# A two-block transformer on one core: sixteen experts at fixed places, three-product weights of 1 MB, and a loop for what overflows

## What is computed

```python
g_logits = (t @ w_group) + b_group                       # 4 groups, the best one is taken
e_logits = ((t @ w_router) + b_router).reshape(-1, 4, 4)
top_p, top_i = lax.top_k(softmax(e_in), 2)               # 2 of the group's 4 experts
w = top_p / sum(top_p) * p_g
hid = silu(einsum('td,edf->etf', t, w_gate)) * einsum('td,edf->etf', t, w_up)
hid = hid * combine.T[:, :, None]
y = einsum('etf,efd->td', hid, w_down)                   # 16 experts: 1024 -> 512 -> 1024
```

## Time and profile before

| what | us |
|---|---|
| median of three executions (range) | 2140.98 (2139.52 to 2141.97) |
| the profiled execution | 2142.71 |
| its span, first to last instruction | 2141.1 |
| PE busy | 1881.8 (88%) |
| DVE busy | 687.8 (32%) |
| ACT busy | 646.3 (30%) |
| first expert product to last (604.5 to 960.5 in the chain) | 356 |

### The profile page before, as it was taken

One profiled execution on the slowest core, in us unless ns is written; L12 is line 12 of the kernel. 1 busy time (PEld: TensorE's weight loads), 2 busy tenths in 40 slices (PEclk: granted clock), 3 DMA queues, 4 the chain that ended last, 5 costly groups with the idle time before them and its releaser, 6 DMA issues.

```text
span 2141.1 us, 21791 instructions
## 1 busy us (share of the span) xinstructions
PE 1881.8 (88%) x8127; PEld 1362.9 (64%) x8127; DVE 687.8 (32%) x1233; ACT 646.3 (30%) x1140; POOL 279.3 (13%) x380
## 2 busy tenths in 40 slices
PE   5996999999479999994999999697777859999996
PEld 4883666667434444443888888585463648888885
DVE  3545334333200000104332332614443262322324
ACT  3224555642110100103221322422546232223222
POOL 2100532310100000001000000423506200000000
PEclk9997999999579999996999999898779879999998
DMA  5226532121279999965332332333000022323321
GB/s 181 83 82 221 189 110 81 60 79 50 93 274 325 344 328 343 325 243 196 99 98 89 99 98 88 97 93 104 1 29 11 30 69 79 98 89 99 99 98 50
DMA packets 210788, 279.53 MB, mean 131 GB/s; under 512 B 9554, under 2 KB 135073, under 8 KB 210576
## 3 DMA queue, kind: packets, MB, share of 16 engines
q1 hardware_dynamic: 198672, 244.35, 34.8%
q0 software_dynamic: 12032, 34.06, 4.4%
HBM read 241.12 MB, written 35.16 MB: 129 GB/s over the span
## 4 chain that ended last, share of the span: by engine, by line
PE 83%; DVE 7%; DMA 3%; issue 2%; POOL 2%; ACT 2%; SPq 0%; DVEq 0%; ACTq 0%; POOLq 0%
PE psum L366 19%; PE psum L367 18%; PE psum L368 18%; PE psum L1059 10%; PE psum L1073 5%; PE psum L505 3%; PE psum L523 3%; PE psum L494 2%; POOL arena L612 2%; DMA warea<-in_w_in 1%; DVE tarea_r L1575 1%; ACT warea_r L351 1%; DVE harea L1547 1%; PE psum L1051 1%; DVE harea L1562 1%
## 5 line engine op out<-in xcount | busy, mean ns | idle before, releaser
L357 DVE TENSOR_TENSOR warea_r<-warea,warea_r 128x2048 fp32r<-128x2048 f32 x114 | 266.5, 2339 | 410.4 <-ACT warea_r L351 410.3
L366 PE MATMUL psum<-tarea_r,warea_r 128*128 128x512 f32 x896 | 356.9, 398 | 12.6 <-DVE tarea_r L1575 12.6
L367 PE MATMUL psum<-tarea_r,warea_r 128*128 128x512 f32 x896 | 351.4, 392 | 0.0
L368 PE MATMUL psum<-tarea_r,warea_r 128*128 128x512 f32 x896 | 351.4, 392 | 0.0
L351 ACT ACTIVATE warea_r<-warea 128x2048 fp32r<-128x2048 f32 x114 | 217.6, 1910 | 308.9 <-PE psum L368 282.4
L1059 PE MATMUL psum<-warea,arena 128*128 128x512 f32 x512 | 225.6, 599 | 0.8 <-ACT arena L1404 0.7
L366 PEld LDWEIGHTS psum<-tarea_r,warea_r 128*128 128x128 f32 x896 | 169.7, 189 | 53.4 <-DVE tarea_r L1575 13.3
L368 PEld LDWEIGHTS psum<-tarea_r,warea_r 128*128 128x128 f32 x896 | 169.7, 189 | 36.4
L367 PEld LDWEIGHTS psum<-tarea_r,warea_r 128*128 128x128 f32 x896 | 169.9, 190 | 33.6
L1059 PEld LDWEIGHTS psum<-warea,arena 128*128 128x128 f32 x512 | 97.1, 192 | 118.2 <-issue 116.7
L366 PE MATMUL psum<-warea_r,tarea_r 128*128 128x512 f32 (+3 forms) x408 | 157.1, 385 | 1.4 <-DVE tarea_r L1953 1.4
(11 more groups left out here) (272 smaller groups left out, 2207.6 us busy)
## 6 DMA issues: line engine op xcount, KB each, us to landing
warea<-in_ffn_w_gu SPq DMA_DIRECT2D x88, 512.0 KB, 5.0
warea<-in_w_gate SPq DMA_DIRECT2D x32, 1024.0 KB, 7.9
warea<-in_w_up SPq DMA_DIRECT2D x32, 1024.0 KB, 7.8
warea<-in_w_down SPq DMA_DIRECT2D x32, 1024.0 KB, 7.1
warea<-in_w_in SPq DMA_DIRECT2D x48, 512.0 KB, 4.7
warea<-in_ffn_w_down SPq DMA_DIRECT2D x40, 512.0 KB, 4.2
x_slots<-arena SPq DMA_DIRECT2D x4, 3072.0 KB, 14.9
arena<-x_slots POOLq DMA_DIRECT2D x17, 512.0 KB, 7.7
```

Source lines behind the costliest of these rows:

```text
L357: dve.tensor_tensor(w_lo[:, u % 2, :], raw[:, u % RAW, :], w_hi[:, u % 2, :].bitcast(f32), ALU.subtract)\
L366: nc.tensor.matmul(out, high, by_high, start=first, stop=False)
L367: nc.tensor.matmul(out, high, by_low, start=False, stop=False)
L368: return nc.tensor.matmul(out, low, by_high, start=False, stop=last)
```

## The change

**Places.** Expert e has block e, whatever its count: slots 128e to 128e + 127. A token whose rank is beyond 128 goes to an overflow block behind the sixteen. `slot_of` and `over_of` are constants for that. Blocks 0 to 14 are written out in every engine's program (`STATIC` = 15) and need nothing from `isml`; block 15 and the overflow blocks are a loop from `STATIC` to `last`. With these inputs the loop runs once, so sixteen blocks are computed, as before.

**Weights.** Each expert is six units of 1 MB: two for gate, two for up, two for down. One DMA loads one unit, and a partition reads one piece of 8 KB (rows p*8 to p*8+3 of the matrix) in place of four of 2 KB. To match it the transposes read `Xb` and `hb` with a step of 8 and 4 elements. There are twelve raw places (`moe_raw`): four in the arena, the two `raw` buffers, four over `hT` and two over `hn`. SP issues units 0 to 3 when the first attention's last product is done, 4 and 5 behind the last units of `w_out`, 6 to 9 when the router's logits are done, 10 and 11 when the scatter is done, and every later one when the unit 12 before it is split. At the end SP waits for the split of unit 77 (`moe_lo` 78) and not for `y_stored` before it feeds the FFN.

**Products.** Every unit is split like the other weights, by ACT and DVE, into the same two buffers `w_hi` and `w_lo`; `XT` and the hidden block are split too. Each fp32 product becomes three of fp32r: a unit is 4 products, 12 matmuls, and a block 72. ACT's `moe_high` for unit n waits for the end of unit n - 2 on PE (`moe_done` n - 1). The copy of the result is shared: ACT the first half, DVE the second.

**Routing.** The counts come before the ranks on PE, the ranks take 4 products and not 10, the slots are signalled (`slots_ready`) before the experts of the overflow blocks, and DVE splits units 0 and 1 before it reads the counts.

The core of the diff:

```diff
-    moe_loaded = [s[f"moe_load{i}"] for i in range(RING)]
+    moe_in = [s[f"moe{i}"] for i in range(12)]
+    moe_raw = ([carve(7168 + 2048 * k, 2048) for k in range(4)] + [raw[:, k, :] for k in range(2)]
+               + [whole(HT_AT + 2048 * k, 2048) for k in range(4)] + [whole(H_AT + 2048 * k, 2048) for k in range(2)])
+    def moe_high(b, i):
+        act, parity = nc.scalar, i % 2
+        n, slot, fills = moe_unit(b, i)
+        act.wait_ge(moe_in[slot], 16 * fills)
+        if not (isinstance(n, int) and n < 2):
+            act.wait_ge(s["moe_done"], n - 1)
+        act.activation(w_hi[:, parity, :], moe_raw[slot], ACT.Copy).then_inc(s["moe_hi"], 1)
+
+    def moe_low(b, i):
+        dve.wait_ge(s["moe_hi"], n + 1)
+        dve.tensor_tensor(w_lo[:, parity, :], moe_raw[slot], w_hi[:, parity, :].bitcast(f32), ALU.subtract)\
+            .then_inc(s["moe_lo"], 1)
...
-            sp.wait_ge(s["y_stored"], 1)
+            sp.wait_ge(s["moe_lo"], 78)
             ffn_half(0, "ffn1", AT_FFN1)
...
-            pool.wait_ge(s["routed"], 1)
+            pool.wait_ge(s["slots_ready"], 1)
...
-            def gate_up(k, i=0):
-                for g in range(2):
-                    moe_arrived(pe, k + g, i)
-                    for c in range(KD):
-                        mm = nc.tensor.matmul(ps[g], XT[:, c, :], wv[:, c, :], start=c == 0, stop=c == KD - 1)
-                    mm.then_inc(s["gu_psum"], 1)
+            def gate_up(b):
+                pe.wait_ge(s["xt_low"], 2 * b + 2)
+                for i in range(4):
+                    n = moe_unit(b, i)[0]
+                    pe.wait_ge(s["moe_lo"], n + 1)
+                    for k in range(4):
+                        c = 4 * (i % 2) + k
+                        mm = products(ps[i // 2], XT_hi[:, c, :], XT_lo[:, c, :], w_hi[:, i % 2, 512 * k:512 * k + 512],
+                                      w_lo[:, i % 2, 512 * k:512 * k + 512], c == 0, c == KD - 1)
+                    mm.then_inc(s["moe_done"], 1)
...
+            def expert_round(b):
+                gate_up(b)
+                slot_features(b + 1)
+                if not (isinstance(b, int) and b == 0):
+                    down(b - 1, 4)
+                hidden_features(b)
```

More of the change, by code:

```diff
@@ L199, in build_blocks @@
     rstd = sb("rstd", [P, 32])
-    small = sb("small", [P, 1000])
+    small = sb("small", [P, 992])
     isml = sb("isml", [P, 64], i32)
@@ L701, in _, with expert @@
             sp.wait_ge(s["routed"], 1)
             last = last_block(sp)
[L703 to L710, removed]
+            def expert(b):
+                return sp.value_load(isml[0:1, ds(b - STATIC + 9, 1)], min_val=0, max_val=NE - 1)
@@ L711, in _ @@
+            with sp.Fori(STATIC, last + 1) as b:
                 e = expert(b)
-                expert_weights(5, "w_gate", e, (s["gu_psum"], 2 * b - 1))
-                expert_weights(6, "w_up", e, (s["gu_psum"], 2 * b))
+                for i in range(4):
+                    expert_unit(b, i, e)
                 before = expert(b - 1)
-                expert_weights(7, "w_down", before, (s["y_psum"], 2 * b - 2))
-            expert_weights(5, "w_down", expert(last), (s["gu_psum"], 2 * last + 1))
+                for i in range(4, 6):
+                    expert_unit(b, i, before)
@@ L718, in ffn_half @@
+            final = expert(last)
+            for i in range(2):
+                n, slot, _ = moe_unit(last + 1, i)
+                sp.wait_ge(s["moe_lo"], 6 * last + i)
+                src = w["w_down"][0][ds(final, 1), :, :].rearrange("o (p c) f -> p (o c) f", p=P)
+                sp.dma_start(moe_raw[slot].rearrange("p (c f) -> p c f", c=2), src[:, 2 * i:2 * i + 2, :])\
+                    .then_inc(moe_in[slot], 16)
             def ffn_half(g, name, at):
@@ new lines, in expert_round @@
+            def expert_round(b):
+                gate_up(b)
+                slot_features(b + 1)
+                if not (isinstance(b, int) and b == 0):
+                    down(b - 1, 4)
+                hidden_features(b)
+            slot_features(0)
+            for b in range(STATIC):
+                expert_round(b)
+            pe.wait_ge(s["routed"], 1)
+            last = last_block(pe)
+            with pe.Fori(STATIC, last + 1) as b:
+                expert_round(b)
+            down(last, 0)
@@ L1416, in _ @@
+                moe_high(b, 5 if zero else 7)
+                act.wait_ge(s["htr_psum"], b + 1)
+                nc.scalar.activation(HT_hi, ps[6].rearrange("p (c q) -> p c q", c=4), ACT.Copy).then_inc(s["hts_ready"], 1)
+                if not zero:
+                    y_high(b - 1, n0 + 6)
+            act.wait_ge(s["mix_psum"], 8)
+            for i in range(2):
+                moe_high(0, i)
+            slot_high(0)
+            for b in range(STATIC):
+                expert_round(b)
             act.wait_ge(s["routed"], 1)
-            slot_copy(0)
```

276 lines of the change are left out of this document (166 added, 110 removed).

## The result

| | before | after |
|---|---|---|
| median of the executions, us (range) | 2141.97 (2139.52 to 2144.29) | 2154.30 (2150.51 to 2155.5) |
| profiled execution, us | 2142.71 | 2150.51 |
| its span, us | 2141.1 | 2148.9 |
| granted clock | 0.931 | 0.931 |

Of five executions of after, one took 3158.22 us at a granted clock of 0.552 and is left out of its median, its range and the ratio. The ratio of after to before is 1.0056, 95% interval 1.0041 to 1.0071: slower by little, but clear of the noise. The forecast was 2134 us; the measured median is 20 us above it, inside the range of 2117 to 2163 and near the price of rival 1, 2157.

What follows compares the result with a forecast made beforehand. Plain fp32 products on PE were taken to bound the expert stage. Terms of -8, +7 and -6.6 us summed to -7.6, so a median of 2134 us, with an 8-in-10 range of 2117 to 2163.

Steps and rivals of the forecast that it cites:

- rival 1: Expert stage: the turn is longer than its links; at 7.8 us the kernel takes 2157 us; chance 0.26.
- What bounds the kernel now: Expert stage before the change: bound by plain fp32 products on PE, 21.91 us a block.
- term 2: Expert stage: the turn through two split buffers sets the pace, 363 us against 355.9, so +7 us.
- term 3: Way from the stage to the first FFN product: halved result copy and less traffic beside the gather, -6.6 us.
- term 1: Way to the first expert product: earlier routing, scatter running alone and landing at 586.5, block load 6 us; -8 us.
- the turn: Expert stage: loop of waits PE, ACT, DVE, PE through one split buffer, 7.31 us per two units, three a block.
- the ends: Ways into and out of the expert stage: -8 us to the first expert product, -6.6 us to the first FFN product.
- The transposes: Expert blocks on PE: reading columns 32 bytes apart costs nothing up to twice 1.3 us; at four times, +27 us.
- The fit: Gather before the FFN: the skill's 2.0 us + bytes / 436 GB/s gives 3.2 us for 512 KB.
- Rival 2: Expert stage: PE's clock falls in the gaps; a third of the stage at 1.2 GHz gives 2190 us; chance 0.08.
- Rivals 4 and 5: Ends of the stage: 4, they give more, turn 7.15, about 2119 us, chance 0.14; 5, nothing, about 2144, 0.10.
- Rival 3: Expert stage: PE sets the pace after all, 17.6 us a block, 2065 us; chance 0.04.

Runs made afterwards that it cites:

- e6: Changed kernel with sixteen blocks written out, no overflow loop, and one plain fp32 matmul per expert product, nothing split; 2129.4 us, ratio to before 0.9934.
- e14: e13 with its third pair of split buffers taken away and nothing else; 2145.1 us, ratio to before 1.0042.
- e7: Changed kernel with SP's first expert unit issued only when slots are known, and DVE's first two splits behind the routing; 2171.9 us, ratio to before 1.0129.
- e9: Changed kernel with DVE's first two splits of expert weights moved from ahead of the routing's arithmetic to behind it; 2151.6 us, ratio to before 1.0049.
- e2: Changed kernel with blocks written out, no overflow loop, and ten raw places in place of twelve; 2150.6 us, ratio to before 1.0064.
- e3: e2 with a third pair of split buffers; 2133.7 us, ratio to before 0.9981.
- e4: e3 with a second buffer for token blocks; 2128.5 us, ratio to before 0.9951.
- e12: e4 with eight gather buffers and DVE's first two splits moved behind the routing; 2125.1 us, ratio to before 0.9934.
- e13: e12 with GpSimd issuing each token block's load a block earlier, ahead of its wait for a result; 2075.4 us, ratio to before 0.9694.
- e10: Changed kernel with eight gather buffers in place of four, so no gather waits for an addition; 2149.3 us, ratio to before 1.0043.

## Why the prediction was wrong

**What bounds the kernel now** was right: plain products at 21.9 us a block in before, and e6, which keeps them, has a stage of 355.8 us.

**The steps that failed.** The forecast sum was -7.6 us and the traces gave +11.0. Of these 18.6 us, 11.2 lie in term 2, 4.3 in term 3 and 3.1 in term 1. With the turn well sized the sum would have been near nothing, -7.6 + 7.2 = -0.4; it takes the token block and the ends as well to come to the measured loss.

**Term 2, the turn mis-sized.** The mechanism was the right one, and so were three of the five links: 1.94, 2.29 and 2.51 us. The two handoffs at the ends of the ring were mis-sized: PE to ACT 732.34 - 731.85 = 0.49 us for 0.42, and DVE to PE's flowing matmuls 0.23 for 0.16: DVE ends at 736.57, PE starts at 736.72, and its second matmul comes at 737.03, 0.08 later than the pace of 0.23. The turn is 7.46 us for 7.31. The 0.42 had been read where ACT starts another instruction, one that reads PSUM, and the 0.05 in the 0.16 behind another of DVE's. The trace of before has the ring's own pairs, with the ring's own sizes: ACT's copy of a unit behind PE (1325.86 - 1325.37 = 0.49), and PE behind DVE's large subtraction, which ends at 183.25 + 2.29 = 185.54, 0.15 before PE starts.

```profile
1325.37 0.39 PE L368 MATMUL psum<-warea_r,arena_r 128*128 128x512 f32 x1
...
1325.86 1.92 ACT L351 ACTIVATE warea_r<-warea 128x2048 fp32r<-128x2048 f32 x1 [8.96 <-PE psum L368]
```

```profile
183.25 2.29 DVE L357 TENSOR_TENSOR warea_r<-warea,warea_r 128x2048 fp32r<-128x2048 f32 x1 [4.16 <-ACT warea_r L351]
...
185.69 0.30 PE L366 MATMUL psum<-warea_r,arena_r 128*62 128x256 f32 x1 [1.65 <-DVE warea_r L357]
```

So nothing in the changed kernel made the handoffs longer; they were read between the wrong pairs. 48 turns of 0.15 us are 7.2 us of the missing 11. About 3 us more are the token block, which the forecast had at no cost because DMA had "no more than now" to move: 374.3 us in after against 371.2 in e14. The remaining 1 us lies in the allowances for the ends. The stage, +18.2, is within the prediction's bounds, which were 8 below and 18 above its +7.

**Rival 1** came out near its price, and in part by luck. It named the deciding turn, 7.47 us, and the changed kernel's block of 22.58 is a turn of 7.53. But its 2157 us was a turn of 7.8 with the full gain at the ends; measured were a shorter turn and half that gain. Of its causes, small work in front of a copy and the strided transposes, e14 shows neither: with both in place its blocks are three turns of 7.46 us and nothing more. I gave it 0.26 because each engine had a third of its time free; but in a ring of waits spare time does not shorten the links.

**Term 1, right but for the load.** The scatter landed at 587.13, 586.5 was forecast, and e7 shows what the early fetch does for it. Counted from the router's first product, at 543.99 us before and 544.96 after, GpSimd starts 29.2 us behind it before and 28.5 after: 0.7 less, as forecast. What the prediction did not see is the room there: DVE's first two splits stand on the routing's path, and e9 and e6 put the worth of taking them away at 5 us of GpSimd's start. One size was off: the load of block 0 took 8.75 us, not 6. In e2, e3, e4, e12, e13 and e14, whose scatters landed 2 to 4 us later, it took 3.5 to 3.7. These have ten raw places, none of them over `hn`, so no unit is issued beside that load, and more units are issued ahead of it. The two exchange with each other, so neither alone says what the crowd costs.

**Term 3, wrong in its bound.** I took the gather as bound by bytes (5.7 us for 2.1 MB less). With the bytes gone, at 256 GB/s and a DMA share of 0.78, the time from the first gather's issue to the last sum's end fell from 20.8 us to 19.1 only. e10 takes the handshake away (eight pieces, four buffers, each reuse waiting for an addition) and has 17.5: eight issues one behind the other take 10.1 us up to the last, whose landing and sum add 7.4. So the issues, the last landing and the handshake were left as the bound. The halved copy gave 0.5 us of the 0.6 forecast.

**The transposes** were costed at nothing, and the Trainium skill's page "SBUF — State Buffer", Door 1, spoke of a penalty for each access that leaves a 16-byte line. In this trace there is hardly one. Eight transposes of after, columns 32 bytes apart, took 1.98 us at half clock (above); at full clock they start 0.111 us apart in after and 0.109 in before. Eight of before at half clock, columns side by side, from its chain of waits at the same place:

```profile
601.91 1.96 PE psum L1051 x8
```

**The fit** of "DMA: Bandwidth & Descriptors" (the Trainium skill, anatomy of a DMA), 3.2 us for 512 KB, was not reached by the gathers, 5.69 and 5.74 us. The store of the last result, alone, took less, 2.92 us. The nearest load is that of block 0 in e13, which took

```profile
591.31 3.47 DMA arena<-x_slots
```

**Rival 2** (the clock falls in the gaps) did not happen: gaps, mostly of 0.8 to 1.7 us, in nearly every turn, and a clock of 1.00. Rivals 4 and 5 are out: the ends gave 7.2 us, between the 20.6 and the 3 that they had, and the stage was not theirs. Rival 3 was true of a kernel a third pair of buffers, a second token block and one earlier issue away (e13, which has eight gather buffers as well).

**Slips in the sums** that changed nothing: two subtractions of DVE are 4.6 us in a turn and not 4.4, and two copies of ACT 3.8 and not 3.6.

## What to carry to other kernels

Where work goes round through several engines and a few buffers, add the links up, and read each handoff between the same pair of instructions that will pass work on in the new kernel: 0.07 us in two of them made 7 of the 18.6 us by which this forecast missed, and the right values stood in the trace of before. A third buffer cut this ring, and only then did the next limit show, a load that one queue issued behind a store; so after each limit removed, look at the waits again before judging the idea. When a gain is forecast from bytes that go away, work out first what bounds the stretch next: the issues, the handshakes, one landing.

## What the runs showed of the hardware

- The clock. With pauses of PE, mostly of 0.8 to 1.7 us, in nearly every turn of 7.46 us the granted clock stayed at 1.00 (after, e14). In e4, after a pause of 4.59 us, transposes and products ran at the lower clock: 0.78 us for a matmul that takes 0.39 a little later, and PEclk was 0.93 in that block. Without any pause, PE busy for 240 of 240 us with fp32r products, it was 1.00 (e13).
- A DMA share near 1 does not say that DMA is the bound. e4 moved 368 GB/s at a share of 0.98 in its short blocks, e13 400 GB/s at 1.00, with PE never waiting.
- A token block of 512 KB, issued when the queues are full of 1 MB units, can need 12 us to land: in e4 issued at 683.97 and landed at 695.99.
